# A gated linear unit by seven products of halves from its third feature block on

## The reference, cut to what matters

```python
ga, gb = jnp.split(jax.nn.gelu(y) @ w_glu + b_glu, 2, axis=-1)
y = ga * jax.nn.sigmoid(gb) * jax.nn.silu(z)
out = y @ w_out
```

## Time and profile before

| what | us |
|---|---|
| median of 3 runs | 1410.69 (1408.85 to 1413.93) |
| the profiled execution, its span from the first to the last instruction | 1411.4 |
| TensorE busy | 1312.1 (93%) |
| DVE busy | 676.0 (48%) |
| ACT busy | 484.0 (34%) |
| POOL busy | 483.8 (34%) |

### The profile page before, as it was taken

How to read it: one execution, slowest core, us unless ns; L and a number is a source line. 1 busy time by engine, 2 the same in 40 slices (tenths; PEclk the granted TensorE clock), 3 DMA queues, 4 the chain that set the end, 5 groups by cost and what they waited for, 6 DMA issues and landing times. The chain is left out here.

```text
span 1411.4 us, 28779 instructions
## 1 busy us (share of the span) xinstructions
PE 1312.1 (93%) x11781; PEld 1235.0 (88%) x11781; DVE 676.0 (48%) x1116; ACT 484.0 (34%) x833; POOL 483.8 (34%) x292
## 2 busy tenths in 40 slices
PE   4998879989889999999999999699999999898997
PEld 4888879989889999999999999599988888788785
DVE  5876678877811121212121100764238777576532
ACT  4223342326442222222222212333345555343531
POOL 2212210000024444444444344043357766665400
PEclk9999999999999999999999999899999999999999
DMA  8468884458533333333333325125255886675601
GB/s 198 91 118 133 141 144 117 134 172 286 207 78 113 104 97 104 98 104 105 105 108 97 90 81 128 31 75 170 77 171 152 275 264 190 225 268 153 237 16 46
DMA packets 248039, 194.22 MB, mean 138 GB/s; under 512 B 44753, under 2 KB 232041, under 8 KB 247185
## 3 DMA queue, kind: packets, MB, share of 16 engines
q1 hardware_dynamic: 247152, 159.48, 42.4%
q10 hardware_dynamic: 800, 33.53, 6.6%
HBM read 172.60 MB, written 53.87 MB: 160 GB/s over the span
## 5 line engine op out<-in xcount | busy, mean ns | idle before, releaser
L109 POOL TENSOR_TENSOR w_lo<-raw,w_hi 128x1024 fp32r<-128x1024 f32 x145 | 347.7, 2398 | 726.0 <-ACT w_hi L104 473.2
L167 PE MATMUL acc<-act_hi,w_hi 128*128 128x256 f32 x1728 | 352.5, 285 | 6.3 <-PEq L444 3.4
L167 PE MATMUL acc<-act_lo,w_hi 128*128 128x256 f32 x1728 | 350.8, 285 | 0.0
L167 PE MATMUL acc<-act_hi,w_lo 128*128 128x256 f32 x1728 | 350.2, 284 | 0.0
L167 PEld LDWEIGHTS acc<-act_hi,w_hi 128*128 128x128 f32 x1728 | 270.2, 190 | 8.7 <-issue 5.7
L167 PEld LDWEIGHTS acc<-act_hi,w_lo 128*128 128x128 f32 x1728 | 270.5, 190 | 0.0
L167 PEld LDWEIGHTS acc<-act_lo,w_hi 128*128 128x128 f32 x1728 | 270.4, 190 | 0.0
L104 ACT ACTIVATE w_hi<-raw 128x1024 fp32r<-128x1024 f32 x149 | 157.6, 1058 | 299.1 <-PE acc L167 256.1
L1399 DVE SCALAR_TENSOR_TENSOR sig<-acc,vec,sig 128x520 f32<-128x520 f32 x16 | 12.2, 760 | 289.6 <-PE acc L167 289.6
L2059 PE MATMUL acc<-act_hi,w_hi 128*128 128x256 f32 (+1 forms) x512 | 112.1, 301 | 12.2 <-ACTq L2379 11.7
L2059 PE MATMUL acc<-act_lo,w_hi 128*128 128x256 f32 (+1 forms) x512 | 104.3, 285 | 0.0
(11 more groups left out here) (324 smaller groups left out, 1936.1 us busy)
## 6 DMA issues: line engine op xcount, KB each, us to landing
raw<-a_w_glu SPq DMA_DIRECT2D x64, 512.0 KB, 4.0
s_kv<-cache_kv ACTq DMA_DIRECT2D x8, 4088.0 KB, 15.8
raw<-a_w_in SPq DMA_DIRECT2D x32, 512.0 KB, 4.3
raw<-b_w_in SPq DMA_DIRECT2D x32, 512.0 KB, 4.3
q_spread<-scratch_q SPq DMA_DIRECT2D x16, 768.0 KB, 7.1
raw<-a_w_out SPq DMA_DIRECT2D x16, 512.0 KB, 4.0
raw<-w_kv SPq DMA_DIRECT2D x16, 512.0 KB, 3.9
k_rows<-cache_kv SPq DMA_DIRECT2D x32, 256.0 KB, 5.2
```

What stands on the lines that cost most here:

```text
L109: pool.tensor_tensor(self.mem.wl[s][:, :, :], self.mem.raw[s][:, :, :], self.mem.wh[s][:, :, :].bitcast(F32), ALU.subtract).then_inc(self. ...
L167: ins = nc.tensor.matmul(mem.acc[a][:, 256 + lo:256 + hi], w[s][:, k, :], x[:, k0 + k, lo:hi], start=first and k == 0 and i == 0, stop=las ...
```

## The change

Blocks 0 and 1 are computed as before. For each of the other 14 blocks the matrix of features x contraction is cut into quarters: `ga` and `gb` for the features, and the first and the second 1024 rows of the contraction (`ga1`, `ga2`, `gb1`, `gb2`, each one raw buffer of 128 x 1024). The activations are cut into contraction halves `y1`, `y2` and token halves of 260. In place of 8 products of quarters there are 7 (Strassen's scheme), 98 in all, each of 24 matmuls of 260 columns. Five of the seven take a sum or difference of two raw blocks as their weights, and five take a sum or difference of activation quarters.

- DVE makes the weight sum of a product (`sum_weights`, 128 x 1024), ACT its high part, and POOL and DVE its low part: POOL slices 0 to 4 (128 x 640), DVE slices 5 to 7 (128 x 384). There are three buffers for products; raw blocks have six.
- The five activation sums are made once, at the start of the stage, in halves of 128 x 1040, while blocks 0 and 1 are multiplied. A half takes one sum of high parts, one copy by ACT, and a chain of three for the low part. DVE makes four of the sums (8 halves), POOL the fifth (2 halves, in between the splits of the plain units).
- A product's result lies in its own PSUM bank, and DVE moves it out with `move`: 12 instructions of 260 columns to a block, each with one operand in PSUM. The sigmoid, the multiplication and the splits of a block come after them. The results wait in fp32 in place of the activations, and `y_hi` and `y_lo` are made in five portions at the end, since the activation sums lie in their place.
- The loops are gone: everything is written out. The next stages swap the numbers of weight buffers; a few semaphores are cleared and used again.

The diff, cut to the steps that the prediction names (`first_sums(q)` is one sum of 128 x 1040 by DVE, `low_sums(q)` a chain of three such operations, `last_sum` POOL's share, `high` and `low` make `y_hi` and `y_lo`):

```diff
+HALF_T = TOK // 2
+PLAIN = 2
+PRODUCTS = (("ga1", ALU.add, "ga2", None), ("ga1", None, None, 0), ("gb1", ALU.subtract, "ga1", 1),
+            ("ga1", ALU.add, "gb2", 2), ("ga2", ALU.subtract, "gb2", 3), ("gb1", ALU.add, "gb2", None),
+            ("gb2", None, None, 4))
+SUMS = ((("y1", 1), ALU.subtract, ("y2", 1)), (("y1", 0), ALU.add, ("y1", 1)), (("y1", 0), ALU.add, ("y2", 1)),
+        (("y2", 0), ALU.add, ("y2", 1)), (("y2", 0), ALU.subtract, ("y1", 0)))
+N_SUM = sum(1 for x in PRODUCTS if x[1])
+BLOCKS = ("ga1", "ga2", "gb1", "gb2")
...
+            for n in range(4, 4 * PLAIN):
+                i, a, u = n // 4, n // 2 % 2, n % 2
+                dn.load(sp, n, u, w[:, 8 * u:8 * u + 8, bass.ds((i + WT) * P - a * W2, P)])
+                if n == 5:
+                    sp.wait_ge(mem.states_stored, 64)
+                    for name in BLOCKS:
+                        load_block(0, name)
...
+            for n in range(3, 4 * PLAIN):
+                dn.split_lo(pool, n, n % 2)
+                for c, x in steps[2 * (n - 3):2 * (n - 3) + 2]:
+                    last_sum(c, x)
+            for n in range(N):
+                split_weights(pool, n, slice(0, 5), w_lo)
...
+            for n in range(N):
+                g, p = divmod(n, 7)
+                t, s = PRODUCTS[p][3], slot(n)
+                if t is not None:
+                    xh, xl = th[t], tl[t]
+                else:
+                    name, half = ("y2", 1) if p == 0 else ("y1", 0)
+                    xh, xl = (part(x, name, half, slice(0, 8)) for x in (act_h, act_l))
+                if g == 0:
+                    if p == 0:
+                        pe.wait_ge(dn.acc_free[0], PLAIN + 1)
+                    if p == 2:
+                        pe.wait_ge(dn.acc_free[1], PLAIN + 1)
+                    if t == 4:
+                        pe.wait_ge(p_sum_lo, 6)
+                    elif t is not None:
+                        pe.wait_ge(y_sum_lo, 6 * t + 6)
+                else:
+                    pe.wait_ge(moved, 7 * (g - 1) + (2, 3, 3, 4, 5, 6, 7)[p])
+                pe.wait_ge(w_lo, n + 1)
+                for k in range(8):
+                    if k == 5:
+                        pe.wait_ge(w_lo_v, n + 1)
+                    for i, (a, x) in enumerate(((wh, xh), (wh, xl), (wl, xh))):
+                        ins = nc.tensor.matmul(banks[p], a[s][:, k, :], x[:, k, :],
+                                               start=k == 0 and i == 0, stop=k == 7 and i == 2)
+                ins.then_inc(multiplied, 1)
...
+            dn.split_hi(act, 3, 1, 1)
+            plain_sigmoid(0, ga)
+            sum_hi(act, 0, 0, y_sum, 1, y_sum_hi)
+            sum_hi(act, 0, 1, y_sum, 2, y_sum_hi)
+            dn.split_hi(act, 4, 0, 2)
+            sum_hi(act, 4, 0, p_sum, 1, p_sum_hi)
+            sum_hi(act, 1, 0, y_sum, 3, y_sum_hi)
+            dn.split_hi(act, 5, 1, 2)
+            sum_hi(act, 1, 1, y_sum, 4, y_sum_hi)
+            sum_hi(act, 2, 0, y_sum, 5, y_sum_hi)
+            dn.split_hi(act, 6, 0, 3)
+            sum_hi(act, 4, 1, p_sum, 2, p_sum_hi)
+            sum_hi(act, 2, 1, y_sum, 6, y_sum_hi)
...
+            for n in range(3, N):
+                weights_hi(n)
+                if n % 7 == 2:
+                    sigmoid(n // 7 - 1)
+                if n >= N - 2:
+                    act.wait_ge(multiplied, n - 3)
+                    j = n - N + 2
+                    high(j, 4 * j, 4 * j + 4)
+            act.wait_ge(multiplied, N - 3)
+            high(2, 8, 12)
+            act.wait_ge(nxt.landed[0], 16)
+            act.wait_ge(multiplied, N - 2)
...
+                a, b = block_at(g, first), block_at(g, second)
+                v.wait_ge(raw_in[a], 16 * turn_of(g, first))
+                v.wait_ge(raw_in[b], 16 * turn_of(g, second))
+                if n >= 3:
+                    v.wait_ge(multiplied, n - 2)
+                elif n > 0:
+                    v.wait_ge(dn.unit_read, 4 * PLAIN + n)
+                v.tensor_tensor(ws[slot(n)][:, :, :], raw[a][:, :, :], raw[b][:, :, :], op).then_inc(summed, 1)
...
+                v.wait_ge(multiplied, n + 1)
+                if n:
+                    v.wait_ge(moved, n)
+                if p == 0:
+                    v.sem_inc(moved, 1)
+                    if g:
+                        gate(g - 1)
+                    return
+                if p == 1:
+                    if g:
+                        v.wait_ge(prod, PLAIN + g)
+                    v.tensor_scalar(ga[:, hi_half], b[0], bias, None, ALU.add).then_inc(begun, 1)
+                    v.tensor_scalar(ga[:, lo_half], b[0], -1.0, bias, ALU.mult, ALU.add)
+                    v.wait_ge(begun, 2 * g + 1)
+                    ins = v.tensor_tensor(ga[:, hi_half], ga[:, hi_half], b[1], ALU.add)
+                elif p == 2:
+                    v.tensor_copy(gb[:, hi_half], b[1]).then_inc(begun, 1)
+                    v.wait_ge(begun, 2 * g + 2)
+                    ins = v.tensor_tensor(gb[:, hi_half], gb[:, hi_half], b[2], ALU.add)
+                elif p == 3:
+                    v.tensor_tensor(ga[:, lo_half], ga[:, lo_half], b[3], ALU.add)
+                    ins = v.tensor_tensor(gb[:, hi_half], gb[:, hi_half], b[3], ALU.add)
+                elif p == 4:
+                    ins = v.tensor_tensor(ga[:, lo_half], ga[:, lo_half], b[4], ALU.add)
+                elif p == 5:
+                    v.tensor_copy(gb[:, lo_half], b[5])
+                    ins = v.tensor_tensor(gb[:, hi_half], gb[:, hi_half], b[5], ALU.subtract)
+                else:
+                    v.tensor_tensor(gb[:, lo_half], gb[:, lo_half], b[6], ALU.add)
+                    ins = v.tensor_tensor(ga[:, lo_half], ga[:, lo_half], b[6], ALU.add)
+                ins.then_inc(moved, 1)
+            def gate(g):
+                i = PLAIN + g
+                v.wait_ge(sig, g + 1)
...
+            first_sums(0)
+            first_sums(1)
+            low_sums(0)
+            first_sums(2)
+            low_sums(1)
+            first_sums(3)
+            plain_gate(0, ga)
+            low_sums(2)
+            first_sums(4)
+            low_sums(3)
+            first_sums(5)
+            sum_weights(0)
+            low_sums(4)
+            split_weights(v, 0, slice(5, 8), w_lo_v)
+            first_sums(6)
+            low_sums(5)
+            split_weights(v, 1, slice(5, 8), w_lo_v)
+            sum_weights(2)
+            plain_gate(1, gb)
+            split_weights(v, 2, slice(5, 8), w_lo_v)
+            v.wait_ge(dn.acc_free[1], PLAIN + 1)
+            store_y(0, ga)
+            store_y(1, gb)
+            first_sums(7)
+            low_sums(6)
+            for n in range(N):
+                if n + 3 < N:
+                    if n + 3 == 3:
+                        v.wait_ge(prod, PLAIN)
+                    sum_weights(n + 3)
+                move(n)
+                if n + 3 < N:
+                    split_weights(v, n + 3, slice(5, 8), w_lo_v)
+                if n == 0:
+                    low_sums(7)
+                if n >= N - 5 and n < N - 1:
+                    j = n - N + 5
+                    low(j, 4 * j, min(4 * j + 4, WT - 1))
+            gate(G_N - 1)
+            low(4, WT - 1, WT)
```

More of the change, by code:

```diff
@@ L76, with __init__ @@
 class Dense:
-    def __init__(self, nc, mem, name, units, first):
+    def __init__(self, nc, mem, name, units, first, slots=(0, 1)):
         def sem(x):
@@ new lines, in _ @@
+            load_z(0)
+            load_z(1)
+            for n in range(4, 4 * PLAIN):
[5 more added lines that the diff above has]
+                        load_block(0, name)
+            for g in range(1, G_N):
+                for name in BLOCKS:
+                    load_block(g, name)
+                load_z(g + 1)
@@ new lines, in _, with y_sum_parts @@
+            load_z(WT - 1)
+            sp.wait_ge(w_lo, 7 * (G_N - 1) + 2)
+            sp.wait_ge(w_lo_v, 7 * (G_N - 1) + 2)
+            for n in range(2):
+                sp.wait_ge(summed, sums_to(7 * (G_N - 1) + 3 + n))
+                sp.dma_start(mem.raw[n][:, :, :], nxt.first[n]).then_inc(nxt.landed[n], 16)
+            nxt.load_second(sp, [w_out[:, 8 * n:8 * n + 8, P:2 * P] for n in range(2)])
+        def y_sum_parts(j, c, low):
+            (xa, ha), op, (xb, hb) = SUMS[j]
+            k = slice(4 * c, 4 * c + 4)
+            x = act_l if low else act_h
+            return part(x, xa, ha, k).bitcast(F32), part(x, xb, hb, k).bitcast(F32), op, k
@@ new lines, in sum_hi, with split_weights @@
+        def sum_hi(act, j, c, ready, count, done):
+            act.wait_ge(ready, count)
+            k = slice(4 * c, 4 * c + 4)
+            act.activation(th[j][:, k, :], tf[j][:, k, :], ACT.Copy).then_inc(done, 1)
+        def split_weights(eng, n, k, done):
+            g, p = divmod(n, 7)
+            name, op = PRODUCTS[p][0:2]
+            s = slot(n)
+            src = ws[s] if op else raw[block_at(g, name)]
+            eng.wait_ge(w_hi, n + 1)
```

(14 more changed lines are left out.)

264 lines of the change are left out of this document (194 added, 70 removed).

## The result

The changed kernel takes 1483.6 us (1483.3 to 1483.7), 1.0508 times the kernel before (95% interval 1.0484 to 1.0532), whose median of four runs is 1411.9. The forecast was 1503.

A forecast was written before the change was run, and what follows sets the result against it. TensorE, 93% busy, was taken to bound the kernel before. Start 86, turns 353, last product 3 and end 8 gave 450 us in place of 357.5: +92.5 on 1411.4, 1504, as a median 1503; range 1421 to 1545.

The forecast's parts named there:

- Direction and cause: Whole kernel: slower, 0.83 likely, mainly because POOL's and DVE's two-operand work add up; this sum alone had 0.62.
- The exclusion of the earlier trace: On DVE and POOL: a two-SBUF-operand DVE operation and a POOL one exclude each other; 22.9 us a block against TensorE's 20.2.
- The signs: In the trace: lengthened DVE sums or POOL low parts, TensorE three quarters busy, blocks of some 26 us, products about 25 later.
- A turn: DVE's work for one product: 4.4 us with a sum, 2.0 without, 3.76 on average; 94 turns make 353 us.
- The 0.3 for the gate: In each block: 0.3 us added to its 26.3 for the gate's splits that meet POOL.
- The start: From the stage's start to the turn preparing product 4: 86 us, bounds 80 to 95, for activation sums under exclusion.
- The end: After the turns: the last product 2.9 us, then 8 (2 to 14) for late low parts and next-stage weights.
- The filled lock: Rival in the turns: sums slip in while POOL waits, so only exclusive time counts; 1421 to 1458 us, chance 0.17.
- The range: Whole kernel: 1421 to 1545 us, holding the sum with its own bounds, 1470 to 1535, and the well-filled rival.
- Faster: Rival at the 98 low parts: POOL's share doesn't hold up DVE, TensorE's 2.88 sets the rate; 1375 us, chance 0.14.
- TensorE's clock: Rival in the products: pauses halve the clock half of the time, products average 4.3 us; 1554 us, chance 0.05.
- At nothing: Terms put at 0: transfers, TensorE's waits, loop-free code, renamed buffers; uncovered loads about 4 x 4, waits up to 3 us.

The follow-up runs named there:

- all_dve: The changed kernel with the low part of each of the 98 products made by DVE alone, none by POOL: 1433.7 us, ratio 1.0157 to the kernel before.
- pool_seven: The changed kernel with POOL making 7 of 8 slices of each low part and DVE 1: 1506.1 us, ratio 1.0681 to the kernel before.
- late_low: The changed kernel with only DVE's order changed: its low-part share is made one turn later, after the next sum: 1454.5 us, ratio 1.0297.
- pool_two: The changed kernel with POOL making 2 of 8 slices, DVE's low parts one turn later, and the start's other two-operand work on DVE: 1415.6 us, ratio 0.9988.
- pool_out: The changed kernel with DVE making all low parts, one turn later, and the start's two-operand work, POOL none: 1431.1 us, ratio 1.0103.

## Why the prediction was right, step by step

- *Direction and cause.* Right. The exclusion of the earlier trace rows sets the turn; `all_dve` and `pool_seven` show it from both sides. The signs came too: the first product began 59.3 us after the stage (482.51), 24.7 later than the 34.6 of the plain tiles, where about 25 were named; TensorE was busy 81% of the stage, where three quarters were.
- *A turn.* 4.4 and 2.0 were forecast, 4.15 to 4.38 and 1.9 measured; a block 24.79, not 26.3. The term was mis-sized in three small places: the two wake-ups on the path took 0.07, not 0.17; DVE's and POOL's low parts together 1.94, not 2.02; and the sum behind POOL 1.08, not 1.15. Of the wake-ups, ACT's was 0.03 and not 0.09 (a figure that stands in no row; the earlier trace rows have 0.14), and what came first behind ACT was DVE after 0.04, while POOL's start took 0.08 as forecast. The 0.3 for the gate was 0.2. Over 94 turns that made 336 us (504.23 to 839.88) in place of 353: 17 of the 22.5 us by which the 1504 for the profiled execution was too high (its span is 1481.5; the median lies 2.1 above that, and 19 below the 1503). The lower bound that was given for a block, 24.6, was nearly the truth, in part by luck: its wake-ups were right, but POOL's bare part takes 1.64 and not the 1.49 put there in proportion, and the gate's 0.3 is left out of it. That DVE would come first was named as a variant of the same total; it was so in most turns.
- *The start.* 86 us forecast, 81.1 measured (423.18 to 504.23). The prediction's exclusive work, called about 81, is 83.4 by the terms that it lists (38.4, 8 and 37). In the trace two-operand work of DVE or POOL is under way in 78.6 us of this time and 2.6 are empty. So the work was put too high, the 5 us for gaps too, and that the whole comes out at the 81 of the work alone is chance. The waits of the plain tiles for POOL, from unit 4 on, were foreseen; all four stand in the rows.
- *The end.* 2.9 and 8 were forecast. The last product ended 1.4 behind its last low part, the pause before the next stage is 2.1, and the next stage's first tile pays 6.1: 9.6 in all. In sum 11 were forecast. What delays the last low parts is inside the turns. No run takes this part on its own.
- *The filled lock* (1421 to 1458) did not come in this kernel. `late_low` moved towards it and stopped at 23.06 a block.
- *The range.* Its own bounds for the sum, 95 + 94 x 28.5 / 7 + 3 + 14, add up to about 1548, not to the 1535 given; the measured time lies far from that end.
- *Faster.* Ruled out as put: POOL's share holds DVE up. Its rate of 20.2 to 20.4 is reached with a smaller share and another order.
- *TensorE's clock.* The granted clock was 0.76 in the stretch of the start where TensorE waited most (457.6 to 504.3), and 0.99 in the turns (0.95 in the stretch from 499 to 600, 1.00 from 600 to 800), with three pauses in each block, of 0.78, 1.53 and 1.06 us. The rival fell. The Trainium skill, "TensorE: Matmul & The Clock Gate", section "HAM oscillation — how this bites in real kernels", speaks of longer pauses; its effect isn't seen in the turns here.
- *At nothing.* What transfers and TensorE's extra waits cost in the changed kernel no row tells apart. Where TensorE is the bound it is little: 1645 matmuls in 200 us in `pool_two` are 0.1216 us each, against 0.120 in the kernel before. That is 0.3 us a block and 4 in all, about the 3 that were named as possible.

## What to carry to other kernels

Before work is shared between DVE and POOL, look in the trace for a two-operand DVE operation next to a POOL operation: if its record is as long as both, the two engines' work adds up, and the share of POOL costs twice what it costs on DVE (2.39 and 1.23 us for 1024 elements). Then the order on DVE counts as much as the amount: a wait for another engine between two such operations can leave a hole that nothing fills. A small share on POOL, in pieces short enough to fall beside DVE's PSUM operations, can still be worth more than none, and work that a scheme needs once at its start needs cover of its own length.

## What was not expected of the hardware

- A short piece on POOL was nearly free where a long one was not. With the same late order a block took 21.54 us with nothing on POOL (`pool_out`), 20.44 with pieces of 256 elements (0.74 us, `pool_two`) and 23.06 with pieces of 640 (`late_low`), though by the exclusive time alone each piece on POOL should cost more than it saves on DVE. The start differs in the last of these, the turns do not. DVE's sums tell where the pieces fall: a median of 1225 ns in `pool_two` and of 1909 in `late_low`, with 1209 bare. No run puts the short pieces elsewhere.
- Taking POOL out altogether and reordering DVE gave nothing over taking POOL out (21.55 and 21.26 us a block), though DVE then had 19.4 us of work to 20.2 of TensorE's.
